# Four edits at once in a two-block transformer kernel: order of the first loads, early splits, two fixed experts, a regrouped attention loop

## The reference, cut to what matters

```
for l in range(2):
    h = rms_norm(x, norm_g[l, 0]);  x = x + 0.5 * swiglu(h, ffn weights [l, 0])      # hidden width 2816
    h = rms_norm(x, norm_g[l, 1]);  q, k, v of three attention branches = h @ w_in[l]
    merged = sum over branches of sigmoid(h @ w_gate[l] + b_gate[l]) * (y_branch @ w_branch[l])
    x = x + merged @ w_o[l]
    h = rms_norm(x, norm_g[l, 2]);  x = x + 0.5 * swiglu(h, ffn weights [l, 1])
x = rms_norm(x, final_g)
```

```
mod = silu(c) @ w_ada + b_ada                      # shifts, scales and gates; also for c_ctx
hx, hc = modulated norms of x and of the context (256 tokens each)
attention: 8 heads of 64, queries from x, keys and values from context and x (512 keys)
retention: 4 heads, decayed scores (q @ k) * D, D from exp(log decay * distance), then group norm and gate
x = x + gate1 * (concat(attention, retention) @ w_out)
h2 = modulated norm of x
each token picks one of 4 groups and 2 of its 8 experts (32 experts in all):
    y = sum of weight * (silu(h2 @ w_gate[e]) * (h2 @ w_up[e])) @ w_down[e]          # hidden width 512
x = x + gate2 * y;   output = rms_norm(x, final_norm_g)
```

## Time and profile before

| | us |
|---|---|
| median of 3 runs | 2302.58 |
| lowest, highest | 2300.70, 2303.02 |
| profiled execution | 2301.19 |
| its span in the profile | 2299.4 |
| PE, DVE, ACT busy | 2113.8, 1194.9, 621.5 |
| mean granted PE clock | 0.966 |

### The profile page before, as it was taken

The page is one execution under the profiler, slowest core; times in us unless marked ns, Lnnn a source line. Parts: engine busy times, 40 slices in busy tenths (PEclk is TensorE's granted clock), DMA queues, the critical chain, the costliest instruction groups (busy, mean ns, idle before and its releaser), DMA issues.

```text
span 2299.4 us, 33997 instructions
## 1 busy us (share of the span) xinstructions
PE 2113.8 (92%) x14044; PEld 1707.2 (74%) x14044; DVE 1194.9 (52%) x2059; ACT 621.5 (27%) x917; POOL 0.2 (0%) x4
## 2 busy tenths in 40 slices
PE   3999999998999999999999899989894899999996
PEld 2999998867999899999878899968564433444443
DVE  3665658873566565656876465553565222222112
ACT  2433434331433433343441333320211000000000
POOL 0000000000000000000000000000000000000000
PEclk8999999999999999999999999999897999999999
DMA  8656563225866566655233576512100999999994
GB/s 228 225 179 203 150 190 110 91 84 171 255 193 211 174 203 211 183 165 165 74 99 112 191 221 212 186 37 75 54 19 21 409 415 416 415 416 416 416 416 188
DMA packets 287098, 471.39 MB, mean 205 GB/s; under 512 B 17386, under 2 KB 223140, under 8 KB 286940
## 3 DMA queue, kind: packets, MB, share of 16 engines
q1 hardware_dynamic: 285884, 466.27, 58.9%
q10 hardware_dynamic: 1056, 2.88, 0.6%
HBM read 467.96 MB, written 1.13 MB: 204 GB/s over the span
## 4 chain that ended last, share of the span: by engine, by line
PE 78%; DMA 12%; DVE 6%; ACT 2%; SPq 1%; issue 1%; DVEq 0%; ACTq 0%
PE ps L572 76%; DMA ring_zone<-in_moe_w_up_dram 10%; DMA W<-in_ffn_w_up_dram 2%; PE ps L846 1%; DVE QK L1734 1%; SPq L522 0%; ACT S L1378 0%; PE ps L1097 0%; DVE mx L1892 0%; DVE hT L1525 0%; DVE WL L1466 0%; ACT WH L1184 0%; SPq L549 0%; DVE xT L1484 0%; DVE S L1897 0%
## 5 line engine op out<-in xcount | busy, mean ns | idle before, releaser
L1466 DVE TENSOR_TENSOR WL<-W,WH 128x1024 fp32r<-128x1024 f32 x372 | 453.1, 1222 | 378.5 <-ACT WH L1184 378.3
L572 PE MATMUL ps<-hh,WH 128*128 128x256 f32 x2128 | 614.1, 289 | 25.5 <-issue 12.1
L572 PE MATMUL ps<-hh,WL 128*128 128x256 f32 x2128 | 605.7, 285 | 0.0
L572 PE MATMUL ps<-hl,WH 128*128 128x256 f32 x2128 | 605.7, 285 | 0.0
L1184 ACT ACTIVATE WH<-W 128x1024 fp32r<-128x1024 f32 x372 | 391.0, 1055 | 516.6 <-PE ps L572 476.8
L572 PEld LDWEIGHTS ps<-hh,WH 128*128 128x128 f32 x2128 | 407.5, 192 | 49.2 <-issue 46.7
L572 PEld LDWEIGHTS ps<-hl,WH 128*128 128x128 f32 x2128 | 407.4, 191 | 0.1
L572 PEld LDWEIGHTS ps<-hh,WL 128*128 128x128 f32 x2128 | 406.9, 191 | 0.0
L572 PE MATMUL ps<-ring_over,XT 128*64 128x512 f32 x896 | 208.3, 597 | 31.4 <-DMA ring_over<-in_moe_w_up_dram 20.1
L572 PE MATMUL ps<-hid_h,WH 128*128 128x256 f32 x704 | 203.8, 290 | 0.0
L572 PE MATMUL ps<-hid_h,WL 128*128 128x256 f32 x704 | 199.1, 283 | 0.0
(11 more groups left out here) (303 smaller groups left out, 2299.9 us busy)
## 6 DMA issues: line engine op xcount, KB each, us to landing
ring_over<-in_moe_w_gate_dram SPq DMA_DIRECT2D x128, 512.0 KB, 14.9
ring_zone<-in_moe_w_down_dram SPq DMA_DIRECT2D x128, 512.0 KB, 15.2
ring_over<-in_moe_w_up_dram SPq DMA_DIRECT2D x96, 512.0 KB, 15.5
W<-in_ffn_w_gate_dram SPq DMA_DIRECT2D x88, 512.0 KB, 5.9
W<-in_ffn_w_up_dram SPq DMA_DIRECT2D x88, 512.0 KB, 4.5
W<-in_ffn_w_down_dram SPq DMA_DIRECT2D x88, 512.0 KB, 3.7
W<-in_w_in_dram SPq DMA_DIRECT2D x78, 512.0 KB, 4.0
ada_w<-in_w_ada_dram SPq DMA_DIRECT2D x48, 512.0 KB, 4.4
```

Of the source, the lines that this page charges most:

```text
L572: ins = nc.tensor.matmul(o, lhsT, rhs, start=start, stop=stop, skip_group_check=True, **kw)
L1466: v.tensor_tensor(low, W[:, i % RAW, :], high.bitcast(F32), ALU.subtract).then_inc(low_ready, 1)
```

## The change

**x first.** The first loads are the 128 columns of the identity, x, and `norm_g`, with a semaphore of their own; PE waits for these. The first pieces follow, and the other setup loads come behind the first 6 pieces on SP or, 15 of them, from ACT's queue. The rest of the vectors, the bucket table and the setup values on DVE are made in block 1 of the first FFN (`late_vectors`), ACT's part in block 2 (`set_up`), DVE's last part in block 3 (`late_factors`). The shifted tables are loaded ahead of pieces 23, 28 and 33, and turned 3 in a block from block 3 on. The 16 small loads of `na_rpb` are one. The modulation units are spread as 4, 7, 7 and 6 over the FFN stages, and from the fifth on they have two buffers.

**Early splits.** After the output projection, `round_and_square` and `update_and_split` run with `ahead=True`: up to three pieces of the next FFN are rounded and two get their low parts while the projection's later banks are still being made.

**First two experts.** Blocks 0 and 1 are always expert 0's first and expert 1's first. Expert 0's further blocks stand behind all others. The first 24 pieces are issued without the table.

**Attention loop.** The scores go to banks 2 and 3 and no longer through `turns`; retention outputs share banks 0 and 1. ACT scales S, DVE inverts one step later, transposes and V products move back one step, 19 steps in all.

The diff, cut to its core:

```diff
@@ places in the stream
+ADA_BLOCKS = (((0, 0), (4, 6, 8, 10)), ((0, 1), (1, 2, 4, 5, 7, 8, 10)), ((1, 0), (1, 2, 4, 5, 7, 8, 10)),
+              ((1, 1), (1, 3, 4, 6, 7, 9)))
+LATE_BLOCK, LATE_TURNS = 1, 2
+STORE_AT, T5_AT, NA_AT = 20, 23, (28, 33)
...
@@ SP: first loads
-            sp.dma_start(C[:, :], I["consts"][:, 0:CONST_KEPT]).then_inc(loads, 16)
...
+            sp.dma_start(C[:, 0:P], I["consts"][:, 0:P]).then_inc(first_loads, 16)
             sp.dma_start(xtok, I["x"][0].rearrange("(a p) n -> p a n", p=P)).then_inc(xload, 16)
...
+            sp.dma_start(vrow[0:48, 0, :], I["norm_g"].rearrange("l i (k p) -> (l i k) p", p=P)).then_inc(first_loads, 16)
...
+            def first_experts(pieces):
+
+                for n in pieces:
+                    if n == RAW:
+                        sp.wait_ge(pair_used, len(split_at))
+                    if n == RING_OVER:
+                        sp.wait_ge(m_ready, 2 * KD + 4)
+                    if n < RAW:
+                        sp.wait_ge(plain_used, plain_no[moe_at - RAW + (n - moe_at) % RAW] + 1)
+                    kind, e, c, half = plan[moe_at + n]
+                    src = piece_source(kind, e, c, half)
+                    tile, loaded, _ = piece_place(moe_at + n)
+                    sp.dma_start(tile.rearrange("p (k n) -> p k n", k=src.shape[1]), src).then_inc(loaded, 16)
...
+                    if plan[i] == ("w_out2", 0, 2, 1):
+                        first_experts(range(RAW, RING_OVER))
...
             stream(0, RAW)
 
+            later_loads()
             sp.wait_ge(pad_ready, due(pad_ready))
-            for l in range(DEPTH):
-                for h in range(NA_H):
-                    at = (l * NA_H + h) * NA_ROWS
-                    sp.dma_start(padt[at:at + NA_ROWS, 48:79], I["na_rpb"][l, h, 4:11, :]).then_inc(pad_load, 16)
+            pads = padt[0:DEPTH * NA_H * NA_ROWS, 48:79]
+            sp.dma_start(pads, I["na_rpb"][:, :, 4:11, :]).then_inc(pad_load, 16)
+            stream(RAW, STORE_AT)
             store_bias_rows()
-            stream(RAW, moe_at)
+            stream(STORE_AT, T5_AT)
+            load_t5()
+            stream(T5_AT, NA_AT[0])
+            load_na(0)
+            stream(NA_AT[0], NA_AT[1])
+            load_na(1)
+            stream(NA_AT[1], moe_at)
+            first_experts(range(RING_OVER, RING))
+            first_experts(range(RAW))
             sp.wait_ge(table_ready, 1)
-            stream(moe_at, rest_at)
+            stream(moe_at + RING, rest_at)
@@ PE: start, late vectors
+            def late_vectors():
+
+                pe.wait_ge(loads, LOADED)
+                bank = begin()
+                nc.tensor.transpose(bank[:, 0:VEC_A], vrow[0:VEC_A, 0, :], ident[0:VEC_A, 0:VEC_A])
+                nc.tensor.transpose(bank[:, 128:128 + VEC_B], vrow[0:VEC_B, 1, :],
+                                    ident[0:VEC_B, 0:VEC_B]).then_inc(work_ready, 1)
+                turns.step()
+                bank = begin()
+                mm(bank[0:12, 0:512], table[:, :], bucket, True, True, then=work_ready)
+                turns.step()
...
-            pe.wait_ge(loads, LOADED)
-            pe.wait_ge(setup, due(setup))
+            pe.wait_ge(first_loads, 32)
...
@@ PE: attention loop
-                    bank = begin()
-                    mm(bank[:, 0:512], QK[base:base + 64, h // 2, q * P:(q + 1) * P],
-                       QK[base:base + 64, kt_:kt_ + 2, :], True, True, then=work_ready)
-                    turns.step()
+                    if s >= 2:
+                        pe.wait_ge(exps, 24 * DEPTH + s - 1)
+                    mm(ps[:, 2 + s % 2, 0:512], QK[base:base + 64, h // 2, q * P:(q + 1) * P],
+                       QK[base:base + 64, kt_:kt_ + 2, :], True, True, then=qk_ready)
...
                 u = s - 1
                 if 0 <= u < 16:
+                    r, kt = u // 4, u % 4
+                    pe.wait_ge(ret_a, due(ret_a))
+                    mm(ps[:, r // 2, (r % 2) * T:(r % 2 + 1) * T], VR[:, kt, r * P:(r + 1) * P], yT[:, 8 + u % 4, :],
+                       kt == 0 and r % 2 == 0, kt == 3, then=acc_ready if kt == 3 else None)
+                u = s - 2
+                if 0 <= u < 16:
                     pe.wait_ge(p_ready, due(p_ready))
...
@@ ACT
                     for k in (2 * b, 2 * b + 1):
                         nc.scalar.activation(hh[:, k, :], xT[:, k, :], ACT.Copy, scale=gain(k)).then_inc(norm_h, 1)
+                    if ahead and b < 3:
+                        halves(free=b + 1)
...
                 if 0 <= s - 1 < 16:
+                    b = (s - 1) % 4
+                    act.wait_ge(rc_ready, due(rc_ready))
+                    nc.scalar.activation(S[:, b, :], S[:, b, :], ACT.Copy, scale=rc[:, b, 0:1]).then_inc(p_ready, 1)
@@ DVE
                 low(0, gain)
                 low(1, gain)
+                if ahead:
+                    rests(free=1)
                 update(2, scale)
                 low(2, gain)
                 low(3, gain)
+                if ahead:
+                    rests(free=2)
                 update(3, scale)
...
-                    dve.wait_ge(exps, due(exps))
-                    give(v.reciprocal(rc[:, b, 0:1], sm[:, b, 0:1]))
-                    given()
-                    v.tensor_scalar(S[:, b, :], S[:, b, :], rc[:, b, 0:1], None, ALU.mult).then_inc(p_ready, 1)
...
+                if 0 <= s - 1 < 16:
+                    b = (s - 1) % 4
+                    dve.wait_ge(exps, due(exps))
+                    v.reciprocal(rc[:, b, 0:1], sm[:, b, 0:1]).then_inc(rc_ready, 1)
...
+            v.tensor_scalar(own_extra[:, :], blocks[:, 0:1], 1.0, -1.0, ALU.max, ALU.add)
+            v.tensor_scalar(own_far[:, :], place[:, :, 0], float(SLOTS), float(SLOTS), ALU.is_ge, ALU.mult)
+            link(v.tensor_scalar(blocks[:, 1:2], blocks[:, 1:2], 1.0, None, ALU.max))
+            link(v.memset(blocks[:, 0:1], 1.0))
...
+            link(v.scalar_tensor_tensor(out=own_at[:, :], in0=upto[:, n - 1:n].to_broadcast([P, TT]), scalar=-1.0,
+                                        in1=own_far[:, :], op0=ALU.add, op1=ALU.mult))
+            link(v.tensor_tensor(slot[:, 0, :, 0], slot[:, 0, :, 0], own_at[:, :], ALU.add))
```

More of the change, by code:

```diff
@@ L395, in build @@
         stored = ev("out_stored")
-        ada_loaded = ev("ada_loaded")
+        ada_loaded = [ev(f"ada_loaded{i}") for i in range(2)]
         ada_used = ev("ada_used")
@@ L755, in _ @@
                 turns.step()
-            bank = begin()
-            mm(bank[0:12, 0:512], table[:, :], bucket, True, True, then=work_ready)
-            turns.step()
-            pe.wait_ge(act_setup, due(act_setup, 3))
+            pe.wait_ge(setup, due(setup))
             for l in range(DEPTH):
@@ L953, in _ @@
             dve_did(turns.n - 1)
-            for s in range(18):
+            for s in range(19):
                 if s < 16:
@@ L977, in _ @@
                     t_idx[u] = turns.step()
[L978 to L982 removed]
+                u = s - 3
                 if 0 <= u < 16:
@@ L1190, in used, with round_and_square @@
                 halves()
-            def round_and_square(gain, early=False):
+            def round_and_square(gain, early=False, ahead=False):
                 for b in range(4):
@@ L1227, in norm, with set_up @@
                 turns.step()
+            def set_up():
+                act.wait_ge(setup, due(setup, 2))
+                nc.scalar.activation(lamt[:, 4:8], lamt[:, 0:4], ACT.Exp)
+                nc.scalar.activation(dect[:, :], dect[:, :], ACT.Exp).then_inc(act_setup, 1)
+                act.wait_ge(act_setup, due(act_setup))
+                nc.scalar.activation(lf[:, :], dect[:, :], ACT.Ln, bias=1.0).then_inc(act_setup, 1)
+                nc.scalar.activation(sc_[:, :, 0], cols("c"), ACT.Silu)
+                nc.scalar.activation(sc_[:, :, 1], cols("c_ctx"), ACT.Silu).then_inc(act_setup, 1)
             def ffn(l, i):
@@ L1485, in update, with update_and_split @@
                                        op0=ALU.mult, op1=ALU.add).then_inc(x_tiles, 1)
-            def update_and_split(scale, gain):
+            def update_and_split(scale, gain, ahead=False):
                 update(0, scale)
@@ L1601, in ffn @@
                         used(2)
-                ada_columns(ada_unit(l, i, FF_BLOCKS - 1))
+                if ada_unit(l, i, FF_BLOCKS - 1) is not None:
+                    ada_columns(ada_unit(l, i, FF_BLOCKS - 1))
                 used(2)
-            v.memset(sc_[:, :, :], 0.0)
+            v.memset(ones[:, :], 1.0).then_inc(setup, 1)
             link(v.memset(padt, 0.0))
```

286 lines of the change are left out of this document (154 added, 132 removed).

## The result

The changed kernel takes 2223.18 us (median of 4 runs, 2220.84 to 2229.06), the kernel before 2302.44 us on the same chip. The ratio is 0.9663, with a 95% interval of 0.9651 to 0.9675: 79 us less. The forecast was 2230.5 with a range of 2221 to 2248, so the time lies inside the range, 7.3 us under the forecast. The profiled execution, the fastest of the four, took 2220.84 us with a span of 2218.9.

A forecast was written before the change was run, and what follows sets the result against it. PE, busy 92% of the span, was taken as the bound, with transfers setting the expert stage's end. Gains 11.9 + 21.1 - 1.5 + 15.6 + 13 + 12.1 = 72.2 us took the profiled 2301.2 to 2229, median 2230.5, range 2221 to 2248.

The forecast's parts named there:

- the expert stage: Routing and experts: first 24 weight pieces loaded before routing, so the stage gains 12.1 us (9 to 13).
- the second border: Second layer's border from output projection to FFN: early splits let PE go on at once, gain 8.3 us.
- the 19.1 us stall: First FFN: PE's wait behind `rs`, caused by bias table loads, goes when they are placed later; gain 21.1 us.
- the rivals with a lost gain: Loop clock stays low (2239 to 2240, chance 0.12), tables stall again (2240, 0.12), experts gain nothing (2242, 0.05).
- the one with the tables: Rival, first FFN: tables stall the weight stream again, only later; half of 19.1 us returns, 2240 us, chance 0.12.
- more than the sum: Rival: flight, borders, loop and experts all at their good ends, 5.9 us more gain, 2225 us, chance 0.05.
- the loop: Second block's attention loop: PE becomes the bound at 3.53 us a step, 61 us in all; gain 13 us (5 to 15).
- the first FFN: First FFN stage: 21.1 us from the stall removed, less 1.5 for work added on PE's path, gain 19.6 us.
- the term of x's flight and the chain behind it: Start: x lands at 6.0 after 4.8 us, 7.8 us of chain follow, FFN at 13.8; gain 11.9 us (10 to 13.5).
- The regrouped modulation units are 24 as before: nothing: FFN stages: modulation units, regrouped but 24 as before, neither gain nor cost time.
- the first decay stall stay, and with it 10.7 us: Attention loop's beginning: first decay stall remains, taking 10.7 us until step 3's scores at half clock.
- DVE needs about as much: Old attention loop: DVE needs about PE's 3.53 us a step, waiting for `exp` and then scaling S, 0.49 us.

The follow-up runs named there:

- experiment 5: Changed kernel with all three shifted bias table loads ahead of piece 20 in place of 23, 28 and 33: 2231.17 us, ratio 0.9703 against the kernel before.
- experiment 1: The changed kernel run again without any edit: 2227.04 us, ratio 0.9681 against the kernel before.
- experiment 9: Changed kernel with ACT rounding piece 0 before the last four `hh`, and DVE making its `WL` behind the first `hl`: 2219.73 us, ratio 0.9652.
- experiment 7: Changed kernel with the attention loop's scaling of S back on DVE, banks and three-step depth kept: 2223.3 us, ratio 0.9666 against the kernel before.
- experiment 3: Changed kernel with the old attention loop put back (one working bank, scaling on DVE, two steps deep): 2246.43 us, ratio 0.9763 against the kernel before.
- experiment 6: Changed kernel with PE waiting for all setup loads again, load order kept: 2236.94 us, ratio 0.9731 against the kernel before.
- experiment 2: Changed kernel without the early splits: 2239.61 us, ratio 0.973 against the kernel before.

## Why the prediction was right, and where it was off

**Right.** All four parts gained, the expert stage by 12.2 us for 12.1, the second border by 8.7 for 8.3, and the 19.1 us stall with its half clock is gone. None of the rivals with a lost gain came about; the one with the tables is real under another condition (experiment 5), and the loop's clock is 1.00 from its 13th us on. The time is nearer to the rival "more than the sum" (2225, chance 0.05) than to the forecast, though not by its terms: the start came out below its range (9.5 against 10 to 13.5), the loop above its own (15.9 against 5 to 15), and what was over came from the loop, the first border, the first FFN and the clock elsewhere.

**Partly luck.** The stages differ from the forecast by errors of both signs: the start and the stretch before the loop gave 3.9 us less, the first FFN, the borders and the loop 8.0 more, and two stages without a forecast 4.1 more, of which at least 2.9 are clock. In experiment 1 the same kernel was 73.2 us faster than the kernel before and not 79.3, so the distance between the forecast of 72.2 and one median is of the size by which the medians themselves move.

**Start: 9.5 for 11.9, the term of x's flight and the chain behind it.** x was issued at 1.19 and landed 5.3 us later, where I took 4.8. The transposes began at 7.03, not at 6.0, held by the row load of `norm_g` (6.8 us of wait), and took 3.68 for 3.45. And the chain left out DVE's eight `hl` operations, 3.25 us, which stand in its program between the copies and the first low split. In the kernel before they were there too, nearly hidden beside `hh` and the high split. Here they hold `WL` for about 1.1 us (an estimate, from experiment 9's rows). The three make up the 2.4 us. Experiment 9 gains more than that, 2.7 us, because it also rounds the first piece sooner on ACT.

**First FFN: 22.35 for 19.6.** This term was 2.75 us small. "The regrouped modulation units are 24 as before: nothing" is true of the sum and false of the stage. The first FFN has four of them now, and the second and third seven each. Counted from start to start at full clock, the first FFN now has 64 matmuls on `ada_a`, 4.0 us, where six units have 96, 6.0 us, and 16 for 24 short ones behind them, some 1.5 for 2.2 us: 2.7 us less for two units, and about 1.5 more in each of the other two. The stages of the second and third FFN gained 2.0 and 0.5 us over their forecasts all the same. A wait of 1.0 us for `rs` in the second is gone, and between the two PE waits 1.9 us for `hl` where it waited 3.8, and its clock stays at 1.00 behind that, where it was 0.71 over the next 9.5 us before. Why `hl` came sooner was not tried.

**Loop: 15.9 for 13.** The forecast was 12.7 us to the fourth step's row maximum, 42.4 for twelve steps, and 6 for the tail and small waits, 61.1 in all (against 74.5 that is a gain of 13.4, put down as 13). By the row maxima the first three steps take 9.5 us, the next twelve 41.7, and the tail 7.4: the mis-sized term is the beginning, by 3.2 us. There I let "the first decay stall stay, and with it 10.7 us"; the wait is still 3.0 us, but with scores in banks of their own the next two row maxima follow 2.83 and 1.38 us behind the first, where they stood 4.36 and 4.57 apart. PE's wait and DVE's row maxima, the first being at 1575.16:

```profile
1576.70 0.67 PE L618 MATMUL ps<-yT,T 128*128 128x256 f32 x2 [3.00 <-DVE rt L2002]
```

```profile
1577.99 0.68 DVE L1996 TENSOR_REDUCE mx<-ps 128x1 f32<-128x512 f32 x1
...
1579.37 0.67 DVE L1996 TENSOR_REDUCE mx<-ps 128x1 f32<-128x512 f32 x1
```

Of the twelve steps, those with both 64-row groups in one half take 3.57 us, near the 3.53 I counted, those in two halves 3.13, and those around a decay up to 4.6, which nearly cancels: 3.47 on average. PE is the bound as forecast. But "DVE needs about as much" named the wrong cause for it: the scaling's move to ACT costs 1.0 us (experiment 7; it takes 0.71 us there, where the nearest row said 0.61), and the depth and the banks carry the gain. The Trainium skill (TensorE: Matmul & The Clock Gate, A second HAM failure mode: psum-queue depth-cycling) tells of a kernel of bf16 matmuls in which cycling through accumulator banks left small idle gaps that made the clock swing. That did not show with the two score banks, since the loop's clock is 1.00 from 1587.8 to its end. In the old loop the half clock came behind waits of 2.7 and 3.9 us for DVE (experiment 3).

**Unforecast.** 2.9 us in the first layer's attention, where nothing was changed: the clock, and by experiment 1 not the change. The stretch before the loop lost 1.5 us (134.5 to 135.0 in all kernels with the early splits, 133.4 without them). That is clock too: PE's waits there are the same, and over the 34 us behind the first of them the mean clock is 0.80 in the changed kernel, its repeat and experiment 6, against 0.85 in the kernel before and in experiment 2. Why it comes back later there was not tried.

## What to carry to other kernels

Before adding up a chain at a start, write down for each engine all that its program puts ahead of the needed instruction; what was hidden before is in the chain once the rest is shorter. A transfer that stalled a stream need not shrink: it is enough to place it where the consumer's stock (here 21 us) is longer than its landing time. Where single executions differ by several us from the clock alone, compare stage lengths between fixed instructions and not spans, and learn first from repeats which stages hold still: here two attention stages and the expert stage moved by 3 to 4 us with the same code. An experiment that moves work on two engines gives the price of both together.

## What the runs showed of the hardware

- Float32 matmuls of 64 rows in different halves of the array overlap: a group of four takes 1.12 us in place of 1.55.
- After equal waits (3.67 and 3.66 us) the same code ran at half clock for about 3 us in one execution and 9 in another; in experiment 3, behind a wait of 2.7 us, a PE that no longer stood was held at 1.2 GHz for 27 us.
- The stretch that read the two `na_scr` tables moved 210 GB/s at a DMA share of 1.05, where expert weights move 415 at 1.03: the engines are as busy for half the bytes.
